# Rotary half turn of the A mixers: from one full-precision product to two one-pass products of parts, with the turn between the halves of the next input piece

## The chip, the cores and the metric

The kernel is one program on one core of a Trainium2 chip. The metric is the device time in microseconds, from repeated executions; a second, separate execution was recorded by the hardware profiler. The engines each run their own queue of instructions in order, and meet at semaphores: TensorE (PE: matmuls, with PEld for its weight loads), VectorE (DVE), ScalarE (ACT), GpSimd (POOL) and SyncE (SP, which issues DMAs).

## The reference, cut to what matters

A stack of fourteen stages on 256 tokens of width 1024 (feed-forwards, a recurrent hybrid, an mLSTM, and attention mixers). The change touches the two differential attention mixers, called A here. Their computation:

```python
def apply_rope(x, cos, sin):                      # on q and k, 16 half heads of 64
    x1, x2 = jnp.split(xf, 2, axis=-1)
    return jnp.concatenate([x1 * c - x2 * s, x2 * c + x1 * s], axis=-1)

def diff_attention(h, w_in, w_out, lam_params, subln_g, cos, sin, layer_idx):
    q, k, v = jnp.split(h @ w_in, [nq, 2 * nq], axis=-1)
    q = apply_rope(...); k = apply_rope(...)
    p = softmax(where(causal, q @ k * scale, -inf))           # two per head
    o = (p[:, :, 0] - lam * p[:, :, 1]) @ v
    o = rms_norm_2(o, subln_g) * (1.0 - lam_init)
    return o.reshape(...) @ w_out
```

The rotation needs, beside x, its half turn: the vector (-x2, x1) within each 64 rows. The kernel makes it as a product with a constant 128x128 matrix of 0, 1 and -1, `turn`.

## The kernel before, in words

**Exactness by parts.** A float32 product on TensorE takes several passes. The kernel mostly splits each float32 operand into a high part of type fp32r, which goes through in one pass, and a low part (the value minus its high part), and sums three one-pass products. For the weights, ScalarE makes the high part (`hi`, L625) and VectorE the low part (`lo_ahead`, L1262). The half turn (L2450) is an exception: it takes the float32 matrix and the float32 values directly.

**The weight stream.** Weights come in pieces of 128x2048 through three slots: SyncE loads piece n when the low part of piece n-3 is made; ScalarE makes its high part when TensorE is done with piece n-3, VectorE then its low part. ScalarE and VectorE work on piece k+2 when their queue reaches the step of piece k.

**An A mixer** has 12 input pieces (8 with queries or keys, each a pair of heads, 4 with values) and 4 output pieces. TensorE projects a piece into one of three banks (`project`; a value piece in `values`), ScalarE copies the result out (`evacuate`), two buffers `raw_qk` in turn. TensorE turns it into the bank MISC (`turn_pair`), and VectorE rotates: raw x cos (L1665), turned x sin (L1668), their sum (L1682), which it signals with `roped`.

**The order of the work** is one string per kind of mixer, `ATTENTION`, walked by TensorE, ScalarE and VectorE alike; each engine puts into its own queue what it has to do at a step. Numbers are pieces, rotations or units (heads):
- `in` k: TensorE projects piece k; ScalarE makes the high part of piece k+2, then copies piece k out; VectorE makes the low part of piece k+2. `fst` and `snd` (used by the C mixer only, before) are the halves: TensorE projects columns 0 to 127 or 128 to 255; ScalarE's high part stands at `fst` and its copy at `snd`.
- `rot` k: TensorE turns, VectorE rotates. The turn waits for the copy, for the rotation before (`roped`) and for the outputs read from MISC.
- `S` u: TensorE computes scores of unit u (it waits for `roped` of the pair's query and key, for example S2 for rotation 3, and for the exponentials of unit u-1); VectorE finds the row maxima (L1734 to L1743, "mask" below); ScalarE makes the exponentials (L916).
- `N` u: VectorE makes the softmax weights (L1753 to L1771) from the exponentials.
- `T` u: TensorE transposes them, ScalarE copies (L926). `W` u: TensorE weighs the values into MISC (L2535, L2536), after waiting for every rotation issued so far; ScalarE copies out (L882).
- `sq`, `sum`, `ln`, `nrm`, `D`, `hi`, `lo`: the norm of the outputs and the output projection.

GpSimd has no work in an A mixer; in the B mixer it makes one high part a unit (L607).

Of the kernel before, what the change touches and what calls it, by code (L numbers as in the profile page):

```python
# [55 lines left out]
for _name, _rows in ROWS:  # L56
# [15 lines left out]
WEIGHTS_MOVE = {"A": 4, "B": 4, "C": 4}  # L72
LATE_LOW = {"A": (), "B": (6, 8), "C": ()}
ATTENTION = {
    "A": """in0 in1 in2 rot0 in3 rot1 in4 S0 rot2 in5 S1 rot3 N0 in6 S2 T0 rot4 N1 in7 W0 S3 T1 rot5 N2 in8 W1 S4 T2 rot6
            N3 in9 W2 S5 T3 rot7 N4 sq0 in10 W3 S6 T4 sum0 N5 ln0 nrm0 sq1 in11 T5 sum1 W4 S7 N6 ln1 D0.0 W5 sq2 hi0 D0.1
            nrm1 T6 N7 D0.2 D0.3 lo0 sum2 W6 ln2 D1.0 D1.1 nrm2 T7 D1.2 D1.3 hi1 lo1 W7 sq3 D2.0 D2.1 sum3 ln3 nrm3
            D2.2 D2.3 hi2 lo2 D3.0 D3.1 D3.2 D3.3 hi3 lo3""",
    "B": """in0 in1 in2 scale0 in3 scale1 U0 in4 in5 scale2 U1 in6 scale3 low8 U2 in7 scale4 U3 in8 scale5 low10 U4 in9 U5 in10 scale6
# [86 lines left out]
def build(nc, a, out, stages):  # L166
# [13 lines left out]
    with ExitStack() as ctx:  # L180
        def sb(name, shape, dt=F32):
            return ctx.enter_context(nc.sbuf_tensor(name, shape, dt))

        def sem(name):
            return ctx.enter_context(nc.semaphore(name))
# [44 lines left out]
        sp_r = sb("sp_r", [P, 4, 384], F32R)  # L230
        sp_hi, sp_lo = sp_r[:, 0:2, :], sp_r[:, 2:4, :]
        pick_r = sb("pick_r", [P, SSD_H], F32R)
        rows_r = sp_r[:, :, :].rearrange("p a c -> p (a c)")[:, 0:2 * T]
        sinks = sb("sinks", [P, 16])
        lam = sb("lam", [P, 2])
# [158 lines left out]
        ln_ready = sem("ln_ready")  # L394
        sp_ready = sem("sp_ready")
        nb_ready = sem("nb_ready")
        sph_ready = sem("sph_ready")
        spl_ready = sem("spl_ready")
        r_ready = sem("r_ready")
        arg_ready = sem("arg_ready")  # L400
# [148 lines left out]
        @block.gpsimd  # L549
        def _(pool):  # L550
            nchain = [0]

            def link(ins):
                nchain[0] += 1
                ins.then_inc(pool_chain, 1)
                pool.wait_ge(pool_chain, nchain[0])

            link(pool.memset(ident[:, :], 0.0))
            pool.memset(ones[:, :], 1.0).then_inc(const_ready, 1)
            pool.memset(eps_c[:, :], EPS).then_inc(const_ready, 1)  # L560
            pool.affine_select(out=ident[:, :], in_=ident[:, :], compare_op=ALU.not_equal, fill=1.0, base=0,
                               pattern=[[-1, P]], channel_multiplier=1).then_inc(const_ready, 1)


            for t in (causal, later):
                link(pool.memset(t[:, :], 1.0))
            for t in (turn, a_mask, c_mask):
                link(pool.memset(t[:, :], 0.0))
            halves = turn[:, :].rearrange("p (h c) -> p h c", h=2)

            def keep(view, op, fill, base, pattern, multiplier):
                link(pool.affine_select(out=view, in_=view, compare_op=op, fill=fill, base=base,
                                        pattern=pattern, channel_multiplier=multiplier))

            keep(causal[:, 0:256], ALU.is_ge, 0.0, 0, [[1, 256]], -1)
            keep(causal[:, 256:384], ALU.is_ge, 0.0, 0, [[1, P]], -1)
            keep(later[:, :], ALU.is_gt, 0.0, 0, [[-1, P]], 1)
            keep(halves[:, :, 0:32], ALU.not_equal, -1.0, -32, [[-64, 2], [-1, 32]], 1)
            keep(halves[:, :, 32:64], ALU.not_equal, 1.0, 0, [[-64, 2], [-1, 32]], 1)
            keep(a_mask[:, 0:256], ALU.is_ge, -1e30, 128, [[-1, 256]], 1)  # L580
            keep(a_mask[:, 256:384], ALU.is_ge, -1e30, 0, [[-1, P]], 1)
            keep(c_mask[:, 0:128], ALU.is_gt, -1e30, 0, [[1, P]], -1)
            keep(c_mask[:, 128:256], ALU.is_ge, -1e30, 0, [[-1, P]], 1)
            keep(c_mask[:, 256:384], ALU.is_ge, -1e30, 0, [[-1, P]], 1)
            link(pool.memset(blocks[:, :], 1.0))
            keep(blocks[:, :], ALU.is_ge, 0.0, 0, [[-4, 32]], 1)
            keep(blocks[:, :], ALU.is_ge, 0.0, 3, [[4, 32]], -1)
            pool.memset(sub_mark[:, :], 0.0).then_inc(masks_ready, 1)
            if plan.subs:
                pool.wait_ge(first_used, 2 * KT - 2)  # L590
                for i, piece in enumerate(ada_pieces):
                    for x in range(2):
                        if i:
                            pool.wait_ge(ada_chain, 2 * (i - 1) + x + 1)
                        pool.dma_start(ada_w[:, x, :], a["ada"][2 * (piece - 8) + x]).then_inc(ada_loaded[x], 16)  # L595


            for st in plan.steps:
                if st["key"][0] == "B":
                    for kind, u in sequence("B"):  # L600
                        if kind != "U":
                            continue
                        if u < 8:
                            pool.wait_ge(sp_ready, u + 1)
                            if u:
                                pool.wait_ge(r_ready, u)
                            pool.tensor_copy(sp_hi, sp).then_inc(sph_ready, 1)  # L607


        @block.scalar  # L610
        def _(act):
# [239 lines left out]
            def evacuate(st, i):  # L851

                kind, n = st["key"][0], st["piece"] + i
                act.wait_ge(piece_used, n + 1)
                b = io(n)
                if kind == "C" and i == 0:
                    act.activation(raw_part(kind, 0)[:, 0, :], b[:, 0, :], ACT.Copy).then_inc(proj_ready, 1)
                    return
                if i in VALUE_PIECES[kind]:
                    if i % 2:  # L860
                        p = VALUE_PIECES[kind][i]
                        for x in range(TB):
                            act.activation(V[:, x, 512 * p:512 * p + 512], IO[(n - 1 + x) % RING][:, :],
                                           ACT.Copy, scale=r_col[:, x:x + 1]).then_inc(proj_ready, 1)
                    return
                rot = ROT_PIECE[kind].index(i)
                query = kind == "C" or rot % 2 == 0
                if kind == "B":
                    j = rot // 2
                    dst = (Q if query else K)[:, 2 * j:2 * j + 2, :]  # L870
                else:
                    buffers = 4 if kind == "C" else 2
                    if rot >= buffers:
                        act.wait_ge(roped, st["rots"] + rot - buffers + 1)
                    dst = raw_part(kind, rot)
                act.activation(dst, b, ACT.Copy, scale=0.125 if query else 1.0).then_inc(proj_ready, 1)

            def outputs(st, u):
# [365 lines left out]
        def _(dve):  # L1244
# [449 lines left out]
            def stick_unit(st, u):  # L1694
# [8 lines left out]
                if u < 8:  # L1703
                    dve.wait_ge(ln_ready, u + 1)
                    if u:
                        dve.wait_ge(spl_ready, u)
                    banks = score_banks(st, u)
                    for h in range(2):
                        ins = dve.scalar_tensor_tensor(out=sp[:, h, :], in0=banks[h][:, 0:384], scalar=0.0,
                                                       in1=lnv[:, h, :], op0=ALU.max, op1=ALU.add)  # L1710
                    ins.then_inc(sp_ready, 1)
                    if u >= 2:
                        dve.wait_ge(o_ready, st["att"] + u - 1)
                    w = nb[:, u % 2, :, :]
                    for h in range(2):
                        ins = dve.scalar_tensor_tensor(out=w[:, h, :], in0=banks[h][:, 0:384], scalar=0.0,
                                                       in1=lnv[:, h, :], op0=ALU.min, op1=ALU.subtract)
                    ins.then_inc(nb_ready, 1)
                    dve.wait_ge(sph_ready, u + 1)
                    if u:  # L1720
                        dve.wait_ge(r_ready, u)
                    dve.tensor_tensor(sp_lo, sp, sp_hi.bitcast(F32), ALU.subtract).then_inc(spl_ready, 1)
# [64 lines left out]
            def attention(st):  # L1787
                kind, n0 = st["key"][0], st["piece"]
                for step, k in sequence(kind):
                    if step == "in" or (step, k) == ("fst", 2):  # L1790
                        if k not in LATE_LOW[kind]:
                            lo_ahead(n0 + k + 2)
                    elif step == "low":
# [387 lines left out]
            def lambda_columns():  # L2181
# [2 lines left out]
                dve.tensor_copy(later_r[:, :], later[:, :])  # L2184
                dve.tensor_copy(ones_r[:, :], ones[:, 0:4])
                link(dve.tensor_copy(ident_r[:, :], ident[:, :]))
                for i in range(2):
                    link(dve.tensor_tensor(lam[:, i:i + 1], lam_s[:, 2 * i + 1:2 * i + 2], lam_s[:, 2 * i:2 * i + 1],
                                           ALU.subtract))
# [29 lines left out]
        def _(pe):  # L2219
# [216 lines left out]
            def turn_pair(st, k, units):  # L2436
# [10 lines left out]
                elif kind == "C":  # L2447
                    pe.wait_ge(ot_ready, st["att"])
                m = MISC[:, 0:nt * T].rearrange("p (t n) -> p t n", t=nt)
                pe.matmul(m, turn[:, :], raw_part(kind, k)[:, 0:nt, :], start=True, stop=True).then_inc(turned, 1)  # L2450

            def scores(st, u):
# [572 lines left out]
```

## Time and profile before

| what | us |
|---|---|
| median of 3 runs | 2405.68 |
| lowest and highest | 2403.62, 2410.78 |
| the profiled execution's own time | 2406.78 |
| its span, first to last instruction | 2404.7 |
| busy: PE, DVE, ACT, POOL | 2345.0, 1718.7, 1192.0, 80.7 |
| granted TensorE clock, mean | 0.997 of full |

The span lies 2.1 us inside the profiled execution's time, and that time is 1.1 us above the median. An instruction's row gives its start and its duration; on TensorE, matmuls overlap, so the time that one takes is read from the start of the next. In brackets stands how long the engine was idle before it, and who ended the wait. The first A mixer lies between about 1172 and 1300 us, the second between about 2088 and 2210.

### The profile page before, as it was taken

How to read it: one execution, taken by the hardware profiler on the slowest of the kernel's cores; microseconds unless marked ns; L12 is line 12 of the kernel's file. 1: busy time of each engine (PE TensorE's matmuls, PEld its weight loads, DVE VectorE, ACT ScalarE, POOL GpSimd, SP SyncE). 2: the span in 40 equal slices, each digit the busy share in tenths (PEclk: the TensorE clock that was granted, in tenths of full speed). 3: DMA queues.
4: the chain of work that ended last, by engine and by line, in shares of the span. 5: the costliest groups of instructions: out<-in, count | busy, mean ns of one | idle time of the engine just before them, and what ended most of it. 6: DMA issues, size and time to landing. Idle time of an engine off the chain costs nothing.

```text
span 2404.7 us, 46561 instructions
## 1 busy us (share of the span) xinstructions
PE 2345.0 (98%) x19290; PEld 2259.5 (94%) x19290; DVE 1718.7 (71%) x2260; ACT 1192.0 (50%) x1489; POOL 80.7 (3%) x163
## 2 busy tenths in 40 slices
PE   6999999999999999999999999999999999999999
PEld 6999988999999989999988999899997899988999
DVE  7888788777877867655677666676667666677665
ACT  5335865334434655433556435654345633546434
POOL 1110000010010000000000000000000000000000
PEclk9999999999999999999999999999999999999999
DMA  8987465787788433455433554436542355443652
GB/s 342 326 314 264 158 217 204 279 295 267 273 297 289 175 135 111 172 194 191 172 123 124 208 192 158 148 116 209 193 175 79 123 204 193 156 153 111 210 192 105
DMA packets 75561, 471.62 MB, mean 196 GB/s; under 512 B 8632, under 2 KB 9144, under 8 KB 26808
## 3 DMA queue, kind: packets, MB, share of 16 engines
q1 hardware_dynamic: 56288, 400.79, 46.5%
q0 software_dynamic: 18432, 67.12, 7.9%
q10 hardware_dynamic: 728, 2.14, 0.3%
q8 instruction: 80, 1.31, 0.2%
q14 instruction: 33, 0.27, 0.0%
HBM read 468.96 MB, written 1.05 MB: 195 GB/s over the span
## 4 chain that ended last, share of the span: by engine, by line
PE 80%; DVE 10%; ACT 4%; DMA 4%; issue 2%; POOL 0%; ACTq 0%; DVEq 0%; POOLq 0%
PE bank L2222 23%; PE bank L2223 23%; PE bank L2224 23%; DVE w_lo L1262 2%; DMA ada_wbuf<-in_ada 2%; PE bank L2228 2%; DVE ada_wbuf L1411 2%; PE bank L2233 2%; PE bank L2229 2%; DMA ARENA<-in_first 1%; ACT w_hi L625 1%; PE bank L2450 1%; PE bank L2484 1%; ACT ARENA L916 0%; DVE ARENA L1734 0%
## 5 line engine op out<-in xcount | busy, mean ns | idle before, releaser
L1262 DVE TENSOR_TENSOR w_lo<-w_raw,w_hi 128x2048 fp32r<-128x2048 f32 x371 | 848.9, 2289 | 319.9 <-ACT w_hi L625 319.1
L625 ACT ACTIVATE w_hi<-w_raw 128x2048 fp32r<-128x2048 f32 x371 | 708.9, 1914 | 508.4 <-PE bank L2224 493.3
L2222 PE MATMUL bank<-h_hi,w_hi 128*128 128x256 f32 x3376 | 944.2, 280 | 1.5 <-DVE w_lo L1262 1.5
L2224 PE MATMUL bank<-h_hi,w_lo 128*128 128x256 f32 x3376 | 935.8, 277 | 0.0
L2223 PE MATMUL bank<-h_lo,w_hi 128*128 128x256 f32 x3376 | 935.8, 277 | 0.0
L2222 PEld LDWEIGHTS bank<-h_hi,w_hi 128*128 128x128 f32 x3376 | 634.7, 188 | 8.3 <-issue 5.1
L2223 PEld LDWEIGHTS bank<-h_lo,w_hi 128*128 128x128 f32 x3376 | 634.8, 188 | 3.5 <-issue 3.3
L2224 PEld LDWEIGHTS bank<-h_hi,w_lo 128*128 128x128 f32 x3376 | 634.6, 188 | 0.0
L2222 PE MATMUL bank<-d_hi,w_hi 128*128 128x256 f32 x1920 | 536.3, 279 | 4.1 <-DVE d_lo L1639 4.0
L2224 PE MATMUL bank<-d_hi,w_lo 128*128 128x256 f32 x1920 | 532.2, 277 | 0.0
L2223 PE MATMUL bank<-d_lo,w_hi 128*128 128x256 f32 x1920 | 532.1, 277 | 0.0
L2222 PEld LDWEIGHTS bank<-d_hi,w_hi 128*128 128x128 f32 x1920 | 360.6, 188 | 7.7 <-DVE d_lo L1639 5.5
L2223 PEld LDWEIGHTS bank<-d_lo,w_hi 128*128 128x128 f32 x1920 | 360.6, 188 | 0.5 <-issue 0.5
L2224 PEld LDWEIGHTS bank<-d_hi,w_lo 128*128 128x128 f32 x1920 | 360.5, 188 | 0.0
L1411 DVE CUSTOM_DVE_ANT_0 ada_wbuf<-ada_wbuf,c_rows 128x1024 f32<-128x1024 f32 x128 | 155.7, 1219 | 31.1 <-DMA ada_wbuf<-in_ada 31.1
L2228 PE MATMUL bank<-h_hi,w_hi 128*128 128x256 f32 x440 | 111.7, 286 | 3.2 <-ACT h_hi L676 2.8
L816 ACT ACTIVATE gate_s<-gate_s 128x512 f32<-128x512 f32 x44 | 27.9, 633 | 170.6 <-DVE gate_s L1572 170.6
L2229 PE MATMUL bank<-h_hi,w_lo 128*128 128x256 f32 x440 | 109.3, 281 | 0.0
L595 POOL DMA_DIRECT2D ada_wbuf<-in_ada x128 | 67.8, 530 | 786.0 <-DVE ada_sum L1411 756.2
L2228 PEld LDWEIGHTS bank<-h_hi,w_hi 128*128 128x128 f32 x440 | 83.5, 190 | 9.4 <-issue 7.7
L789 ACT ACTIVATE gate_s<-bank 128x512 f32<-128x512 f32 x40 | 24.0, 600 | 137.1 <-PE bank L2224 134.8
L1593 DVE CAST d_hi<-hid 128x512 fp32r<-128x512 f32 x88 | 37.5, 426 | 73.8 <-PE bank L2224 73.3
(407 smaller groups left out, 2271.9 us busy)
## 6 DMA issues: line engine op xcount, KB each, us to landing
w_raw<-in_ws SPq DMA_DIRECT2D x371, 1024.0 KB, 4.8
ada_wbuf<-in_ada POOLq DMA_DIRECT2D x128, 512.0 KB, 5.3
ARENA<-in_first SPq DMA_DIRECT2D x8, 1024.0 KB, 19.8
work<-in_x SPq DMA_DIRECT2D x1, 1024.0 KB, 11.3
ARENA<-in_wax ACTq DMA_DIRECT2D x1, 1024.0 KB, 4.8
out_y<-ARENA SPq DMA_DIRECT2D x4, 256.0 KB, 2.2
ARENA<-in_wg ACTq DMA_DIRECT2D x1, 768.0 KB
c_rows<-in_c SPq DMA_DIRECT2D x1, 512.0 KB, 4.9
```

The costliest lines, as they stand in the source:

```text
L595: pool.dma_start(ada_w[:, x, :], a["ada"][2 * (piece - 8) + x]).then_inc(ada_loaded[x], 16)
L625: act.activation(w_hi[:, slot, :], w_raw[:, slot, :], ACT.Copy).then_inc(hi_ready, 1)
L816: act.activation(gate_s[:, :, :], gate_s[:, :, :], ACT.Silu).then_inc(silu_ready, 1)
L1262: dve.tensor_tensor(w_lo[:, s, :], w_raw[:, s, :], w_hi[:, s, :].bitcast(F32), ALU.subtract).then_inc(lo_ready, 1)
L1411: dve.tensor_tensor_reduce(out=w, in0=w, in1=c_rows[:, :], scale=1.0, scalar=0.0, op0=ALU.mult, op1=ALU.add, accum_out=dst).then_inc(ada_c ...
L1593: dve.tensor_copy(d_hi[:, buf, :, :], hid[:, :, :]).then_inc(dve_chain, 1)
L2222: pe.matmul(o, whi, xhi, start=start, stop=False, skip_group_check=True)
L2223: pe.matmul(o, whi, xlo, start=False, stop=False, skip_group_check=True)
L2224: return pe.matmul(o, wlo, xhi, start=False, stop=stop, skip_group_check=True)
L2228: pe.matmul(o, whi, xhi, start=start, stop=False, skip_group_check=True)
L2229: pe.matmul(o, wlo, xhi, start=False, stop=False, skip_group_check=True)
L2233: return pe.matmul(o, whi, xlo, start=False, stop=stop, skip_group_check=True)
```

## The change

The eight rotations of an A mixer work on parts. ScalarE copies each query or key piece twice out of its bank: once as float32, as before, and once rounded to fp32r (the high part). GpSimd subtracts the high part from the float32 copy (the low part). TensorE multiplies an fp32r copy of the matrix, `turn_r`, with the high part and then with the low part, one pass each, into the same bank. The parts lie in `sp_r`, the B mixer's scratch: two buffers for the high part, one for the low part. The order string changes from piece 5 to piece 9: these pieces are projected in halves, and turns 2 to 6 stand between them (turn 2 inside piece 5 and so on); turn 7 stays behind T3. VectorE's low part of piece k+2 is issued at `fst` k, and N0 now stands ahead of rotation 3. One semaphore is renamed, since both kinds of mixer count on it.

```diff
--- before.py
+++ after.py
@@ -72,8 +72,8 @@
 WEIGHTS_MOVE = {"A": 4, "B": 4, "C": 4}
 LATE_LOW = {"A": (), "B": (6, 8), "C": ()}
 ATTENTION = {
-    "A": """in0 in1 in2 rot0 in3 rot1 in4 S0 rot2 in5 S1 rot3 N0 in6 S2 T0 rot4 N1 in7 W0 S3 T1 rot5 N2 in8 W1 S4 T2 rot6
-            N3 in9 W2 S5 T3 rot7 N4 sq0 in10 W3 S6 T4 sum0 N5 ln0 nrm0 sq1 in11 T5 sum1 W4 S7 N6 ln1 D0.0 W5 sq2 hi0 D0.1
+    "A": """in0 in1 in2 rot0 in3 rot1 in4 S0 fst5 rot2 snd5 S1 fst6 N0 rot3 snd6 S2 T0 fst7 rot4 N1 snd7 W0 S3 T1 fst8 rot5 N2 snd8
+            W1 S4 T2 fst9 rot6 N3 snd9 W2 S5 T3 rot7 N4 sq0 in10 W3 S6 T4 sum0 N5 ln0 nrm0 sq1 in11 T5 sum1 W4 S7 N6 ln1 D0.0 W5 sq2 hi0 D0.1
             nrm1 T6 N7 D0.2 D0.3 lo0 sum2 W6 ln2 D1.0 D1.1 nrm2 T7 D1.2 D1.3 hi1 lo1 W7 sq3 D2.0 D2.1 sum3 ln3 nrm3
             D2.2 D2.3 hi2 lo2 D3.0 D3.1 D3.2 D3.3 hi3 lo3""",
     "B": """in0 in1 in2 scale0 in3 scale1 U0 in4 in5 scale2 U1 in6 scale3 low8 U2 in7 scale4 U3 in8 scale5 low10 U4 in9 U5 in10 scale6
@@ -230,6 +230,8 @@
         sp_r = sb("sp_r", [P, 4, 384], F32R)
         sp_hi, sp_lo = sp_r[:, 0:2, :], sp_r[:, 2:4, :]
         pick_r = sb("pick_r", [P, SSD_H], F32R)
+        turn_r = sb("turn_r", [P, P], F32R)
+        raw_parts = sp_r[:, :, :].rearrange("p a c -> p (a c)").rearrange("p (x t n) -> p x t n", x=3, t=2)
         rows_r = sp_r[:, :, :].rearrange("p a c -> p (a c)")[:, 0:2 * T]
         sinks = sb("sinks", [P, 16])
         lam = sb("lam", [P, 2])
@@ -394,7 +396,7 @@
         ln_ready = sem("ln_ready")
         sp_ready = sem("sp_ready")
         nb_ready = sem("nb_ready")
-        sph_ready = sem("sph_ready")
+        gpsimd_part = sem("gpsimd_part")
         spl_ready = sem("spl_ready")
         r_ready = sem("r_ready")
         arg_ready = sem("arg_ready")
@@ -596,6 +598,13 @@
 
 
             for st in plan.steps:
+                if st["key"][0] == "A":
+                    for k in range(8):
+                        pool.wait_ge(proj_ready, st["evac"] + ROT_PIECE["A"][k] + 1)
+                        if k:
+                            pool.wait_ge(turned, st["rots"] + k)
+                        pool.tensor_tensor(raw_parts[:, 2, :, :], raw_part("A", k), raw_parts[:, k % 2, :, :].bitcast(F32),
+                                           ALU.subtract).then_inc(gpsimd_part, 1)
                 if st["key"][0] == "B":
                     for kind, u in sequence("B"):
                         if kind != "U":
@@ -604,7 +613,7 @@
                             pool.wait_ge(sp_ready, u + 1)
                             if u:
                                 pool.wait_ge(r_ready, u)
-                            pool.tensor_copy(sp_hi, sp).then_inc(sph_ready, 1)
+                            pool.tensor_copy(sp_hi, sp).then_inc(gpsimd_part, 1)
 
 
         @block.scalar
@@ -873,6 +882,11 @@
                     if rot >= buffers:
                         act.wait_ge(roped, st["rots"] + rot - buffers + 1)
                     dst = raw_part(kind, rot)
+                if kind == "A":
+                    act.activation(dst, b, ACT.Copy, scale=0.125 if query else 1.0)
+                    if rot > 1:
+                        act.wait_ge(turned, st["rots"] + rot - 1)
+                    dst = raw_parts[:, rot % 2, :, :]
                 act.activation(dst, b, ACT.Copy, scale=0.125 if query else 1.0).then_inc(proj_ready, 1)
 
             def outputs(st, u):
@@ -1716,7 +1730,7 @@
                         ins = dve.scalar_tensor_tensor(out=w[:, h, :], in0=banks[h][:, 0:384], scalar=0.0,
                                                        in1=lnv[:, h, :], op0=ALU.min, op1=ALU.subtract)
                     ins.then_inc(nb_ready, 1)
-                    dve.wait_ge(sph_ready, u + 1)
+                    dve.wait_ge(gpsimd_part, 8 + u + 1)
                     if u:
                         dve.wait_ge(r_ready, u)
                     dve.tensor_tensor(sp_lo, sp, sp_hi.bitcast(F32), ALU.subtract).then_inc(spl_ready, 1)
@@ -1787,7 +1801,7 @@
             def attention(st):
                 kind, n0 = st["key"][0], st["piece"]
                 for step, k in sequence(kind):
-                    if step == "in" or (step, k) == ("fst", 2):
+                    if step == "in" or (step == "fst" and (kind == "A" or k == 2)):
                         if k not in LATE_LOW[kind]:
                             lo_ahead(n0 + k + 2)
                     elif step == "low":
@@ -2184,6 +2198,7 @@
                 dve.tensor_copy(later_r[:, :], later[:, :])
                 dve.tensor_copy(ones_r[:, :], ones[:, 0:4])
                 link(dve.tensor_copy(ident_r[:, :], ident[:, :]))
+                link(dve.tensor_copy(turn_r[:, :], turn[:, :]))
                 for i in range(2):
                     link(dve.tensor_tensor(lam[:, i:i + 1], lam_s[:, 2 * i + 1:2 * i + 2], lam_s[:, 2 * i:2 * i + 1],
                                            ALU.subtract))
@@ -2447,6 +2462,11 @@
                 elif kind == "C":
                     pe.wait_ge(ot_ready, st["att"])
                 m = MISC[:, 0:nt * T].rearrange("p (t n) -> p t n", t=nt)
+                if kind == "A":
+                    pe.wait_ge(gpsimd_part, 16 * st["key"][1] + k + 1)
+                    pe.matmul(m, turn_r[:, :], raw_parts[:, k % 2, :, :], start=True, stop=False)
+                    pe.matmul(m, turn_r[:, :], raw_parts[:, 2, :, :], start=False, stop=True).then_inc(turned, 1)
+                    return
                 pe.matmul(m, turn[:, :], raw_part(kind, k)[:, 0:nt, :], start=True, stop=True).then_inc(turned, 1)
 
             def scores(st, u):
```

## Rows read from the trace of the kernel before

**Rows 1.** Page, part 1: busy us of each engine, share of the span, instructions.

```profile
PE 2345.0 (98%) x19290; PEld 2259.5 (94%) x19290; DVE 1718.7 (71%) x2260; ACT 1192.0 (50%) x1489; POOL 80.7 (3%) x163
```

**Rows 2.** Waits of PE, 1180 to 1262: waiter <- releaser: total, times, longest.

```profile
PE bank L2450 <- ACT scrap L839: 0.6, 1, 0.6
```

**Rows 3.** Timeline of PE: start, duration, instruction; value piece, then a turn.

```profile
1192.55 0.40 PE L2223 MATMUL bank<-w_lo,h_hi 128*128 128x512 f32 x1
1192.78 0.40 PE L2224 MATMUL bank<-w_hi,h_lo 128*128 128x512 f32 x1
...
1205.71 1.02 PE L2450 MATMUL bank<-ARENA,turn 128*128 128x512 f32 x2
...
1206.68 0.28 PE L2223 MATMUL bank<-h_lo,w_hi 128*128 128x256 f32 x1
1206.81 0.28 PE L2224 MATMUL bank<-h_hi,w_lo 128*128 128x256 f32 x1
```

**Rows 4.** Timeline of ACT: copies of pieces 0, 1 and 4; first exponentials.

```profile
1183.60 1.08 ACT L876 ACTIVATE ARENA<-bank 128x512 f32<-128x512 f32 x2 [3.60 <-PE bank L2233]
...
1204.62 0.60 ACT L876 ACTIVATE ARENA<-bank 128x512 f32<-128x512 f32 x1 [3.43 <-PE bank L2224]
1207.30 0.47 ACT L916 ACTIVATE ARENA<-bank,ARENA 128x256 f32<-128x256 f32 x1 [2.08 <-DVE ARENA L1743]
```

**Rows 5.** Timeline of POOL in the B mixer: its cast.

```profile
1516.21 0.82 POOL L607 CAST sp_r<-ARENA 128x768 fp32r<-128x768 f32 x1 [653.74 <-DVE ARENA L1709]
```

**Rows 6.** DVE timeline: mask 0, low 7; rotation 3, N0, low 8, mask 2.

```profile
1205.91 1.15 DVE L1734 TENSOR_REDUCE ARENA<-bank 128x1 f32<-128x256 f32 x4 [2.40 <-PE bank L2489]
...
1210.85 2.29 DVE L1262 TENSOR_TENSOR w_lo<-w_raw,w_hi 128x2048 fp32r<-128x2048 f32 x1 [1.66 <-ACT w_hi L625]
...
1214.97 0.69 DVE L1665 TENSOR_TENSOR ARENA<-ARENA,hid 128x512 f32<-128x512 f32 x1
...
1216.91 0.17 DVE L1753 RECIPROCAL ARENA<-ARENA 128x4 f32<-128x4 f32 x1
...
1218.65 2.29 DVE L1262 TENSOR_TENSOR w_lo<-w_raw,w_hi 128x2048 fp32r<-128x2048 f32 x1
...
1221.51 1.15 DVE L1734 TENSOR_REDUCE ARENA<-bank 128x1 f32<-128x256 f32 x4 [0.57 <-PE bank L2489]
```

**Rows 7.** Timeline of DVE: mask 3, low 10, mask 4.

```profile
1230.30 1.15 DVE L1734 TENSOR_REDUCE ARENA<-bank 128x1 f32<-128x256 f32 x4 [1.18 <-PE bank L2489]
...
1235.63 2.29 DVE L1262 TENSOR_TENSOR w_lo<-w_raw,w_hi 128x2048 fp32r<-128x2048 f32 x1 [0.33 <-ACT w_hi L625]
...
1239.09 1.15 DVE L1734 TENSOR_REDUCE ARENA<-bank 128x1 f32<-128x256 f32 x4 [1.17 <-PE bank L2489]
```

**Rows 8.** Timeline of PE: W0, S3 and T1, one after the other.

```profile
1228.16 0.59 PE L2535 MATMUL bank<-ARENA 128*128 128x256 f32 x2
...
1228.90 0.71 PE L2484 MATMUL bank<-ARENA 64*128 64x256 f32 x4
...
1230.10 0.49 PE L2559 MATMUL bank<-ident,ARENA 128*128 128x128 f32 x3
```

**Rows 9.** PE behind three waits, and windows with busy us and granted clock (PEclk).

```profile
41.10 0.74 PE L2233 MATMUL bank<-h_lo,w_hi 128*128 128x256 f32 x4 [2.67 <-DVE h_lo L1483]
...
1844.03 1.52 PE L2559 MATMUL bank<-ident,ARENA 128*128 128x128 f32 x6 [2.33 <-issue]
...
1854.62 0.85 PE L2559 MATMUL bank<-ident,ARENA 128*128 128x128 f32 x6 [1.57 <-ACT ARENA L885]
...
42.00:43.00 1.00, 1.00 (x7) 1.00 (x6) 0.55 (x2) 0.98 (x2) 0.00 (x0) 0.50 1.01 410
...
1844.00:1845.00 1.00, 0.97 (x5) 1.00 (x6) 1.00 (x3) 0.00 (x0) 0.00 (x0) 0.50 0.01 0
...
1847.00:1848.00 1.00, 1.00 (x7) 0.44 (x4) 1.00 (x4) 1.00 (x7) 0.00 (x0) 0.83 0.00 0
...
1855.00:1856.00 1.00, 1.00 (x14) 0.83 (x13) 1.00 (x3) 0.00 (x0) 0.00 (x0) 1.00 0.00 0
```

## The prediction

> **What bounds the kernel now.** The page first: TensorE is busy for 98% of the span, VectorE for 71% [rows 1]. So a TensorE microsecond taken away is worth one, and so is a TensorE wait that is added. The change touches the two A mixers only; I read the first from its timelines, and take the second as equal (its mask steps stand at the same spacing). Then the waits of TensorE in its first 82 us: one, of 0.6 us, at the first turn [rows 2]. From there past piece 9 it never waits: every other engine has slack there, and the question is how much of it the new order uses up.
>
> **The turn on TensorE.** Before, a turn runs as two instructions that begin at 1205.71; the third matmul behind it begins at 1206.68, and matmuls of this kind follow at 0.12, so the turn took 1206.68 - 0.12 - 1205.71 = 0.85 us. A one-pass product with 512 columns is in the trace: in the value pieces they follow each other at 0.23 us [rows 3]. Two of them cost 0.47. That saves 0.38 a turn, 16 turns: **6.1 us, if nothing waits**. Cutting a piece into halves costs nothing: the same matmuls in the same order, one turn between them.
>
> **ScalarE and GpSimd.** Each of the 16 copies out of the bank is made a second time: 0.60 us by its row [rows 4]. For pieces 4 to 9 it lies in ScalarE's idle time ahead of the next mask (2.1 us idle before the exponentials at 1207.30). The one place where it shows is piece 0: piece 2 may enter bank 0 only when the parts of piece 0 are copied, and here ScalarE goes straight from the end of piece 1 to them; I charge 0.5 us a stage (bounds 0 and 0.6). The subtraction on GpSimd has no row. Nearest: its cast of 768 columns, 0.83 us [rows 5]. 512 columns of one input would be 0.55, doubled for a second input 1.1; I take 1.1, being the nearer case, with 0.55 and 2.3 (as slow as VectorE's subtraction of 2048 columns) for the range. The part is there 0.2 + 0.6 + 0.6 + 0.1 + 1.1 = 2.6 us after the piece ends; the turn comes a score and a half piece later, 1.2 + 2.8 = 4.0. Hidden for turns 2 to 6; at 2.3 us it would be just hidden. Turn 7 keeps its old place behind piece 9 and 2.3 us of other work, and would wait 0.3; but TensorE waits ahead of it anyway (below). The copy of the turning matrix and the renamed semaphore: nothing.
>
> **The move that decides: VectorE's queue.** The order string is walked by all engines. On VectorE an opening half now issues the low part of weight piece k+2, so "S0 fst5 rot2" means mask 0, low 7, rotation 2, where it was mask 0, rotation 2, low 7. Low 7 waits for high 7 from ScalarE, and that stands behind the exponentials of mask 0, which wait for the mask. Before, rotation and softmax weights filled this hole. Now they stand behind it. Terms, start to start [rows 6]: mask to low part 1210.85 - 1205.91 = 4.94; low part 2.20 (2.29 long, 0.09 overlapped); rotation 1216.91 - 1214.97 = 1.94; weights N 1218.65 - 1216.91 = 1.74.
>
> First leg, counted from the start of mask 0. TensorE is never late for S1 (mask 1 may start as soon as VectorE is free): low 7 at 4.94, rotation 2 at 7.14, mask 1 at 9.08, low 8 at 14.02, N0 at 16.22, rotation 3 at 17.96, done at 19.9. S2 needs rotation 3. TensorE would be at S2 after fst, turn, snd, S1, fst, turn, snd, about 13.2: **it waits 6.7 us**. S2 takes 1.20 and a signal 0.2: mask 2 at 21.4. Before it was at 1221.51 - 1205.91 = 15.6. **Lost: 5.8.**
>
> Then three equal cycles. With the transposes in ScalarE's queue, mask to low part is 1235.63 - 1230.30 = 5.33 [rows 7]. Then low part 2.20, rotation 1.94, signal 0.1; W (the weighing with values) waits for all rotations issued so far, so W is next, 0.74, and S 1.20 [rows 8], signal 0.2: 11.7 us from mask to mask, with N beside W and S. Before: 1239.09 - 1230.30 = 8.79. **Lost: 2.9 a cycle, 3 cycles (S2 to S5), 8.8**, as waits of about 3.3 us ahead of W0, W1 and W2. TensorE's savings on turns 2 to 6 only lengthen these waits. After S5 the order is the old one, TensorE sets the pace again.
>
> Per stage: 5.8 + 8.8 + 0.5 at piece 2 - 3 x 0.38 (turns 0, 1, 7) = 14.0; two stages: **+28 us**.
>
> **The clock.** Eight waits of TensorE, two of 6.7 and six of 3.3, are new. The trace has two waits of that size in its running part: 2.67 us before 41.10 and 2.33 before 1844.03. Behind both the granted clock is 0.50, the 1.2 GHz level; the second time it begins with the work at 1844.0 and ends in the window 1847 to 1848, whose mean of 0.83 puts the end at 1847.3 (a third of that window at half), some 3.3 us; after the wait of 1.57 before 1854.62 it stays at 1.00 [rows 9]. Behind W0 and W1, W and S (1.94 us) lie in VectorE's loop, and at half clock with a start 0.5 late they cost 1.4 more; S2 costs 0.7 more; behind W2 TensorE is the bound again and loses 1.7. Sum 0.7 + 1.4 + 1.4 + 1.7 = 5.2 a stage if all four gaps bring it, 10.4 in two. I take three quarters, **8 us**, since 3.3 is not far from the 1.57 that brought none. The Trainium skill (TensorE: Matmul & The Clock Gate, "What's actually happening") says that the lowered clock is the default and sustained activity releases it; by that rule all eight gaps are candidates (+10.4), and the trace agrees at the two gaps named.
>
> **Sum.** The profiled execution took 2406.8 (span 2404.7); 2406.8 + 28 + 8 = 2442.8. It lies 1.1 above the median of the runs, so against 2405.7: **2441 us**, slower by 1.5%.
>
> **Rivals.**
> (a) The waits come, the clock stays up: 2405.7 + 28 = 2434. For: gaps around 3.3 us are rare in this trace and could fall either way; against: both comparable ones brought it. 0.25.
> (b) The two engines get in each other's way: the subtraction starts about 1.4 us after a half piece ends, which in the three cycles is when VectorE adds up the rotation, on the path. If one waits for the other's 1.1 us, six times: +6.6, 2448. The trace can't tell: GpSimd's casts [rows 5] stand beside VectorE instructions that read a bank. The Trainium skill (SBUF — State Buffer, "Who interferes with whom") states that a VectorE instruction with two SBUF inputs and a GpSimd one that reads SBUF exclude each other; it speaks for this rival and nothing in the sum uses it. 0.10.
> (c) Not slower: the hole is no hole. If ScalarE's high part were ready before the mask, the chain mask, low part, rotation, W, S would be 1.3 + 2.2 + 1.9 + 0.1 + 0.7 + 1.2 + 0.2 = 7.6, under TensorE's 8.4 a cycle, and only the turns count: 2405.7 - 6.1 + 1.0 = 2400.6. It decides where the wait for the high part falls under 1.7 us instead of 4.0. For it: VectorE still idles for 0.6 to 1.7 us ahead of single instructions [rows 6]. Against: the high part is queued behind the exponentials, and the low parts in rows 6 and 7 already wait on it. 0.09, a third of it with some further gain.
> (d) Something longer than all this, above 2452: 0.05.
> The forecast has 0.51.
>
> **Numbers.** 0.3% is 7.2 us, about what can be told from no change. Even the full saving of 6.1 is below it, so faster gets 0.03, same 0.06, slower 0.91. The range leaves out (c) and (d): low 2427, which is (a) with one microsecond less in each loop; high 2452, which is (b) with all gaps at half clock.
>
> **What would show it.** Right: waits of TensorE at S2 (near 6.7 us) and W0 to W2 (near 3) on VectorE's rotation add, masks 2 to 5 some 11.7 to 13 apart, VectorE idle about 4 us ahead of low 9, 10 and 11 on ScalarE's high part, turns of 0.47. Wrong: if TensorE waits instead at the turns, for GpSimd, the parts are the bound; if the masks stay 8.8 apart, (c) holds; if the waits are there and the clock row is at 1.00 behind them, (a).

## The result: 2452.2 us against 2405.1, slower by 1.85%

| | before | after |
|---|---|---|
| median of the runs, us | 2405.13 (4 runs) | 2452.16 (4 runs, 2447.33 to 2455.82) |
| ratio, 95% interval | | 1.0185 (1.0171 to 1.0198) |
| span of the profiled execution, us | 2404.7 | 2454.0 |
| first A stage, us | 111.5 | 133.9 |
| second A stage, us | 111.1 | 132.8 |

A stage is measured from one sum of squares to the next: the product of `work` with ones that ends the first pieces of the stage, to that of the feed-forward behind it. The two stages hold 22.4 + 21.7 = 44.1 us of the 47.0. The rest of the run between them is equal (802.7 and 802.3 us). In the profiled execution the first A stage also begins 5.6 us later, 1189.2 against 1183.6. The profiled executions of the experiments have this start anywhere from 1180.5 to 1187.9, ahead of anything that the change issues but one small copy, so I count no part of it for the change.

The page's busy line, to be held against [rows 1]: no engine has more than 24 us of new work, TensorE's busy time rises by 12 in a span longer by 49, and its share falls to 96%.

```profile
PE 2356.9 (96%) x19290; PEld 2273.1 (93%) x19290; DVE 1727.3 (70%) x2261; ACT 1199.6 (49%) x1505; POOL 104.4 (4%) x179
```

The waits of TensorE after, 1180 to 1290 (waiter <- releaser: total, times, longest), where [rows 2] had 0.6 us in all. L2504 is S2, L2555 are W0 to W2, L1696 is the add that ends a rotation on VectorE; L2467 is turn 0:

```profile
PE bank L2555 <- DVE ARENA L1696: 10.8, 3, 4.5
PE bank L2504 <- DVE ARENA L1696: 7.7, 1, 7.7
PE bank L2467 <- issue: 0.5, 1, 0.5
```

TensorE after, a turn between the halves of piece 5, then S2 behind its wait, and the ends of the stage. The turn is 0.47 long (1213.64 to 1214.11), where [rows 3] had 0.85:

```profile
1189.22 1.03 PE L2335 MATMUL bank<-work,ones 128*128 128x256 f32 x4
...
1213.64 0.40 PE L2467 MATMUL bank<-sp_r,turn_r 128*128 128x512 f32 x1
1213.87 0.40 PE L2468 MATMUL bank<-sp_r,turn_r 128*128 128x512 f32 x1
1214.11 0.28 PE L2237 MATMUL bank<-h_hi,w_hi 128*128 128x256 f32 x1
...
1232.25 1.23 PE L2504 MATMUL bank<-ARENA 64*128 64x256 f32 x4 [7.74 <-DVE ARENA L1696]
...
1323.11 1.03 PE L2342 MATMUL bank<-work,ones 128*128 128x256 f32 x4
```

VectorE after, first A stage. L1748 opens a mask, L1276 is a low part, L1696 the rotation's add, L1679 its first product, L1778 two small products in N:

```profile
1211.01 1.15 DVE L1748 TENSOR_REDUCE ARENA<-bank 128x1 f32<-128x256 f32 x4 [2.01 <-PE bank L2509]
...
1215.95 2.29 DVE L1276 TENSOR_TENSOR w_lo<-w_raw,w_hi 128x2048 fp32r<-128x2048 f32 x1 [3.59 <-ACT w_hi L634]
...
1219.48 1.07 DVE L1696 TENSOR_TENSOR ARENA<-ARENA 128x512 f32<-128x512 f32 x1
...
1227.82 1.08 DVE L1778 TENSOR_TENSOR ARENA<-ARENA,lam 128x1 f32<-128x1 f32 x2
...
1234.67 1.15 DVE L1748 TENSOR_REDUCE ARENA<-bank 128x1 f32<-128x256 f32 x4 [2.47 <-PE bank L2509]
...
1239.99 2.29 DVE L1276 TENSOR_TENSOR w_lo<-w_raw,w_hi 128x2048 fp32r<-128x2048 f32 x1 [3.97 <-ACT w_hi L634]
...
1243.52 1.43 DVE L1696 TENSOR_TENSOR ARENA<-ARENA 128x512 f32<-128x512 f32 x1
...
1247.71 1.15 DVE L1748 TENSOR_REDUCE ARENA<-bank 128x1 f32<-128x256 f32 x4 [1.04 <-PE bank L2509]
...
1256.56 1.71 DVE L1696 TENSOR_TENSOR ARENA<-ARENA 128x512 f32<-128x512 f32 x1
...
1268.18 1.78 DVE L1679 TENSOR_TENSOR ARENA<-ARENA,hid 128x512 f32<-128x512 f32 x1
```

The reader is to see three things. Mask to low part is 4.94 and 5.32 us, as in [rows 6, 7], but now VectorE idles 3.6 to 4.0 of it, on ScalarE's high part. Masks 2 and 3 are 13.04 apart, where [rows 7] had 8.79. Masks 4 and 5 are 14.75 apart, which is outside the 11.7 to 13 of the prediction; there the product of 1.78 and the half clock come together. And some instructions are far longer than before: 1.07, 1.43 and 1.71 for an add that always took 0.69, as all 20 of it in the kernel before show (min, median, max in ns):

```profile
L1682 DVE TENSOR_TENSOR ARENA<-ARENA x20: 691/692/694, 1193.5 to 2164.4; 128x512 f32<-128x512 f32 x20
```

GpSimd after: the subtractions of the parts. The one at 1243.15 ends at 1244.41, and the add that began beside it at 1243.52 ends at 1244.95, 0.54 behind it:

```profile
1218.29 1.72 POOL L606 TENSOR_TENSOR sp_r<-ARENA,sp_r 128x512 fp32r<-128x512 f32 x1 [6.11 <-ACT sp_r L890]
...
1243.15 1.26 POOL L606 TENSOR_TENSOR sp_r<-ARENA,sp_r 128x512 fp32r<-128x512 f32 x1 [14.33 <-ACT sp_r L890]
...
1268.15 1.26 POOL L606 TENSOR_TENSOR sp_r<-ARENA,sp_r 128x512 fp32r<-128x512 f32 x1 [10.42 <-ACT sp_r L890]
```

Windows after (busy us of each engine, PEclk, DMA share, GB/s), to be held against [rows 9]: half clock at S2, full again at 1237; half clock behind W2 as well.

```profile
1234.00:1235.00 1.00, 1.00 (x6) 1.00 (x6) 0.33 (x1) 0.00 (x0) 0.00 (x0) 0.50 0.00 0
1237.00:1238.00 1.00, 1.00 (x11) 1.00 (x10) 0.00 (x0) 1.00 (x6) 0.00 (x0) 1.00 0.00 0
1273.00:1275.00 2.00, 2.00 (x11) 1.62 (x10) 0.00 (x1) 0.38 (x1) 0.00 (x0) 0.50 0.00 0
```

### The profile page after: what moved, and what is told of

It reads as the page before. It is cut to its first block, busy times and chain, and to the rows that moved or that the text cites. A ratio compares the mean times of both kernels' runs of the same rounds, so it can differ in the third digit from the quotient of the medians.

```text
span 2454.0 us, 46618 instructions
## 1 busy us (share of the span) xinstructions
PE 2356.9 (96%) x19290; PEld 2273.1 (93%) x19290; DVE 1727.3 (70%) x2261; ACT 1199.6 (49%) x1505; POOL 104.4 (4%) x179
## 4 chain that ended last, share of the span: by engine, by line
PE 74%; DVE 12%; ACT 5%; DMA 4%; issue 4%; POOL 0%; ACTq 0%; DVEq 0%; POOLq 0%
PE bank L2237 21%; PE bank L2239 21%; PE bank L2238 21%; DMA ada_wbuf<-in_ada 3%; DVE w_lo L1276 3%; DVE ada_wbuf L1425 2%; ACT w_hi L634 2%; PE bank L2243 2%; PE bank L2248 2%; PE bank L2244 1%; DMA ARENA<-in_first 1%; ACT ARENA L930 1%; DVE ARENA L1748 1%; PE bank L2504 1%; DVE ARENA L1696 0%
## 5 line engine op out<-in xcount | busy, mean ns | idle before, releaser
L1276 DVE TENSOR_TENSOR w_lo<-w_raw,w_hi 128x2048 fp32r<-128x2048 f32 x371 | 848.9, 2289 | 356.3 <-ACT w_hi L634 355.4
```

Of the source, the lines that this page charges most:

```text
L1276: dve.tensor_tensor(w_lo[:, s, :], w_raw[:, s, :], w_hi[:, s, :].bitcast(F32), ALU.subtract).then_inc(lo_ready, 1)
```

## Experiments

The stage lengths of every profiled execution, first and second A stage, by the same two products; the difference is against 111.5 and 111.1. Each length comes from one profiled execution. The two stages of a kernel agree within 0.4 us, but for the changed kernel and the one with no read on GpSimd (1.1 and 1.3), whose half clock falls differently in the two, while the whole run spreads by up to 11.5 us; so the small effects are read from the stages.

| kernel | median us (ratio to before, interval) | A stages, us | both, against before |
|---|---|---|---|
| after | 2452.2 (1.0185, 1.0171 to 1.0198) | 133.9, 132.8 | +44.1 |
| order alone | 2442.5 (1.0151, 1.0135 to 1.0168) | 129.2, 129.1 | +35.7 |
| no read on GpSimd | 2441.4 (1.0141, 1.0126 to 1.0155) | 129.9, 128.6 | +36.0 |
| waits filled | 2438.6 (1.0136, 1.0118 to 1.0155) | 128.0, 128.1 | +33.5 |
| parts alone | 2416.2 (1.0036, 1.0023 to 1.0049) | 114.6, 114.6 | +6.6 |
| low part at the second half | 2405.4 (0.9996, 0.9986 to 1.0007) | 110.2, 110.4 | -2.0 |
| high part early | 2406.0 (0.9998, 0.9987 to 1.0009) | 110.8, 111.0 | -0.8 |
| parts for six turns | 2402.96 (0.9989, 0.9978 to 0.9999) | 109.1, 109.1 | -4.4 |

**The order alone.** The kernel before, with the diff's string and its VectorE step; no parts.

```diff
-                    if step == "in" or (step, k) == ("fst", 2):
+                    if step == "in" or (step == "fst" and (kind == "A" or k == 2)):
```

> The kernel before with only the new order string and the low part at the first half; the turn is the float32 product of 0.85 us, one copy by ScalarE, nothing on GpSimd. Theory 1: nearly all of the loss is here: waits of 6 at S2 and 2.9 at W0 to W2 a stage, 2 x 14.6 = 29 us, and 4 to 8 us of half clock behind them: 2434 to 2442. Rival (order and parts each carry a share): under 2425.

Measured 2442.5, half a microsecond above the 2434 to 2442 expected. Its waits of TensorE, 1180 to 1330:

```profile
PE bank L2535 <- DVE ARENA L1682: 7.2, 3, 2.9
PE bank L2484 <- DVE ARENA L1682: 5.7, 1, 5.7
```

The order alone loses 35.7 us without a single part. S2 waits 5.7 where the kernel with parts and no read on GpSimd (below) waits 6.5, and W1 and W2 2.9 where that one waits 3.3: two turns and one turn that are 0.38 longer fill the difference. The rest, up to the 7.7 of the changed kernel, is the meeting of GpSimd and VectorE.

**The parts alone.** The changed kernel with the old string (the diff's lines of the string taken back).

> The changed kernel with the order string of before: whole pieces, each turn directly behind one score. Parts by ScalarE and GpSimd stay. The part is ready 0.2 + 0.6 + 0.6 + 0.1 + 1.3 = 2.8 us after the piece, TensorE is at the turn after 1.2 (turns 2 and 3), 1.5 (turn 4) and 2.3 us (turns 5 to 7): waits of 1.6, 1.6, 1.2, 0.5, 0.5, 0.5, and 0.5 at piece 2, in sum 6.4 a stage, less 8 x 0.38 = 3.1: 2 x 3.3 = +6.5, 2411.5 us. Rival (the parts are the dear side of the change): above 2425. Other rival (GpSimd's part comes in time): 2400.

Stages +6.6, which is the expected sum; the median is +9.2, and the interval of the ratio holds 5.5 to 11.8 us. The single waits came out shorter than expected, 4.7 in all for 5.9, so the sum agrees partly by luck, and about 1 us a stage is not accounted for. Its waits of TensorE, 1200 to 1262:

```profile
PE bank L2467 <- POOL sp_r L606: 4.7, 6, 1.3
```

Behind one score, the part comes late. So the halves were needed; what was wrong was what else the string moved.

**The low part at the second half.** The changed kernel, one line of VectorE's.

```diff
-                    if step == "in" or (step == "fst" and (kind == "A" or k == 2)):
+                    if step == "in" or (step, k) == ("fst", 2) or (step == "snd" and kind == "A"):
```

> The changed kernel with one edit: VectorE makes the low part of piece k+2 at the second half of piece k, so behind rotation and softmax weights, as in the kernel before; turns, parts and halves stay. Theory 1 (VectorE's queue makes the waits): the waits at S2 and W0 to W2 are gone, masks 8.4 us apart, 12 turns of 0.47 hidden by nothing; only a second copy at piece 2 (+0.5 a stage) and turn 7's wait for GpSimd (+0.5 a stage) remain: 2405.1 - 6.1 + 2.0 = about 2401 us, under the kernel before by 0.1 to 0.25%. Rival (the parts are the cost, through GpSimd and the second copy): the waits stay in good part, at the turns instead, and the time stays above 2430. If VectorE and GpSimd hold each other up as in the changed kernel, it is slack that pays, and the time is still near 2401.

2405.4: the whole loss is gone, by one step of VectorE's queue, the low part, moved behind others. The gain is -2.0 where -4.1 was expected. The missing 2.1 us is one wait, of turn 7, 1.5 us a stage where 0.5 was expected. In its trace the subtraction for turn 7 starts 0.94 us into a low part and then takes 2.5 us (VectorE, GpSimd, and the wait of TensorE, 1200 to 1262):

```profile
1244.32 2.28 DVE L1276 TENSOR_TENSOR w_lo<-w_raw,w_hi 128x2048 fp32r<-128x2048 f32 x1
```

```profile
1245.26 2.47 POOL L606 TENSOR_TENSOR sp_r<-ARENA,sp_r 128x512 fp32r<-128x512 f32 x1 [5.89 <-ACT sp_r L890]
```

```profile
PE bank L2467 <- POOL sp_r L606: 1.5, 1, 1.5
```

The low part ends at 1246.60; 1.13 us later, at 1247.73, the subtraction is done, a little under its undisturbed length of 1.26. The subtractions for turns 5 and 6 are as long (2.50 and 2.51), but TensorE does not wait for them.

**The high part early.** The changed kernel, VectorE's order and all; ScalarE makes its high part behind the copy instead of behind the exponentials.

```diff
                     elif step == "fst":
-                        hi_ahead(n0 + k + 2)
+                        if kind != "A":
+                            hi_ahead(n0 + k + 2)
                     elif step == "snd":
                         evacuate(st, k)
+                        if kind == "A" and k < 9:
+                            hi_ahead(n0 + k + 3)
```

and the same for piece 7 behind the copy of piece 4.

> The changed kernel, VectorE's order and all; only ScalarE makes its high parts earlier: that of piece k+3 right behind its copy of piece k, so ahead of the exponentials, for pieces 7 to 11. VectorE's low part at the first half then finds its high part ready. Theory (what opens the hole in VectorE's queue is the high part behind the exponentials, as the rival of the prediction that would have ended not slower has it): the chain mask, low, rotation, W, S is 7.7 us, under TensorE's 8.4, the waits at S2 and W0 to W2 are gone: about 2405. Rival (the low part ahead of the rotation costs by its own 2.2 us too): waits of 1 us or so stay at W0 to W2, 2410 to 2415.

2406.0, and masks 8.4 us apart (VectorE, masks 3 and 4 and the low part between them; here no wait for the high part is left, and ahead of low parts 7 and 8 it is 0.3):

```profile
1231.69 1.15 DVE L1753 TENSOR_REDUCE ARENA<-bank 128x1 f32<-128x256 f32 x4 [1.21 <-PE bank L2514]
1232.95 2.29 DVE L1281 TENSOR_TENSOR w_lo<-w_raw,w_hi 128x2048 fp32r<-128x2048 f32 x1
...
1240.08 1.15 DVE L1753 TENSOR_REDUCE ARENA<-bank 128x1 f32<-128x256 f32 x4 [1.20 <-PE bank L2514]
```

A wait of 1.5 us on the rotation stays at S2, which the expectation did not have. So the low part ahead of the rotation does little harm by its own 2.2 us. The harm was that it waited.

**No read on GpSimd.** GpSimd writes zeros and reads nothing from SBUF.

```diff
-                        pool.tensor_tensor(raw_parts[:, 2, :, :], raw_part("A", k), raw_parts[:, k % 2, :, :].bitcast(F32),
-                                           ALU.subtract).then_inc(gpsimd_part, 1)
+                        pool.memset(raw_parts[:, 2, :, :].bitcast(F32), 0.0).then_inc(gpsimd_part, 1)
```

> The changed kernel, but GpSimd fills the low part with zeros instead of subtracting: it reads nothing from SBUF, and the low half of the turn is left out of the result. Same order, same signals. Theory 2 (the subtraction and VectorE's instructions with two SBUF inputs hold each other up, 4.1 us in the first A stage by the lengthened rows: adds of 1.07, 1.43 and 1.71, a product of 1.78 where 0.69 is normal, small products of 1.08 for 0.23): every one of these rows is back at its normal length and the time falls by about 8 us, to 2444. Rival (the lengthened rows come from elsewhere, such as the DMA stream, or are made up for by the waits): they stay, or the time moves by under 2 us. The waits at S2 and W0 to W2 stay in either case, near 6.5 and 3.0.

2441.4 where 2444 was expected; the stages are shorter than those of the changed kernel by 8.1 in all, which is the 8 expected. The rotation's add, all 20 of it (min, median, max in ns), and the waits of TensorE, 1180 to 1330:

```profile
L1695 DVE TENSOR_TENSOR ARENA<-ARENA x20: 691/692/694, 1191.7 to 2198.0; 128x512 f32<-128x512 f32 x20
```

```profile
PE bank L2554 <- DVE ARENA L1695: 9.2, 3, 3.3
PE bank L2503 <- DVE ARENA L1695: 6.5, 1, 6.5
```

In the changed kernel the longest was 1712. The fill is shorter than the subtraction, 0.52 us, but it too runs beside this add (from 2167.30 and 2192.12), and the add keeps its length. The theory stands. Its size is 8.1 us of the 44.1 by the stages, and 7.0 by the lengthened rows, 4.1 in the first stage and 2.9 in the second (small products of 1.08; adds of 1.07, 1.04, 1.23 and 1.48). The 1.1 us between the two is not isolated: the half clock falls at other places in each execution.

**The waits filled.** The changed kernel with idle products ahead of its four waits a stage.

```diff
+            def fill(n):
+                for _ in range(n):
+                    pe.matmul(PS[3][:, 0:T], ident[:, :], causal[:, 0:T], start=True, stop=True)
...
+                    if kind == "A" and (step, k) == ("S", 2):
+                        fill(15)
+                    elif kind == "A" and step == "W" and k < 3:
+                        fill(6)
```

> The changed kernel with float32 products of two constants put into TensorE's queue ahead of S2 (15 of 0.43 us) and ahead of W0, W1 and W2 (6 of 0.43 us), into a bank that nothing uses there, so that TensorE is not idle while it waits for the rotation. Nothing else changes, no result does. Theory (the half clock behind the waits costs 3.4 us in the loops of the first A stage by its rows, and about as much after the last wait and in the second stage): the granted clock stays at 1.00 in both A stages and the time falls by 6 to 9 us against the changed kernel, to 2443 to 2446, with VectorE's rotation still the releaser. Rival (the clock costs nothing, since the work behind a wait has slack): 2452, the clock at 1.00 or not. If the filling is longer than the waits it adds time, by its rows at most 1 us a stage.

2438.6: 13.6 less than the changed kernel by the medians, 11.8 by the ratios to the kernel before, 10.6 by the stages; all are more than the 6 to 9 expected. The clock stays up where W0 and S3 run, and W0 waits for what the fill left over:

```profile
1237.00:1239.00 2.00, 1.80 (x13) 1.51 (x14) 1.66 (x8) 0.39 (x1) 0.00 (x0) 1.00 0.94 393
```

```profile
1237.19 0.67 PE L2555 MATMUL bank<-ARENA 128*128 128x256 f32 x2 [1.04 <-DVE ARENA L1696]
```

Not all of it is clock. The meeting of GpSimd and VectorE also fell otherwise: the lengthened rows of the first stage add 2.3 us here (adds of 1.07 and three of 1.04, small products of 1.09), against 4.1 in the changed kernel. That leaves 5.9 - 1.8 = 4.1 us of clock in the first stage. The second has the same 2.3 against 2.9, and leaves 4.7 - 0.6 = 4.1 too.

**Parts for six turns.** The kernel with the low part at the second half; turns 0 and 7 go back to one copy and the float32 product.

```diff
-                if kind == "A":
-                    pe.wait_ge(gpsimd_part, 16 * st["key"][1] + k + 1)
+                if kind == "A" and 0 < k < 7:
+                    pe.wait_ge(gpsimd_part, 14 * st["key"][1] + k)
```

with the same condition at ScalarE's second copy and in GpSimd's loop.

> The kernel with the low part at the second half (2405.4 against 2407.0), and turns 0 and 7 made as before, with the float32 product and one copy. In its trace turn 7 waits 1.5 us for GpSimd's part, and piece 2 waits 0.5 us for the second copy of piece 0; each of these turns saves 0.38 as parts. Theory: a stage gains 1.5 - 0.38 + 0.5 - 0.38 = 1.3 us on it, two stages 2.5: 2402.9, and against the kernel before -2.0 - 2.5 = -4.5 us (0.9981). Rival: the waits only pass on to the next ones, S5 to S6 or the value pieces: no difference from 2405.4.

Stages -4.4, where -4.5 was expected, and median 2402.96. The ratio says less: 0.9989 where 0.9981 was expected. Its interval, 0.9978 to 0.9999, holds the expected one and just leaves out no change. Its waits of TensorE, 1190 to 1262, hold none for GpSimd:

```profile
PE bank L2469 <- ACT scrap L847: 0.6, 1, 0.6
PE bank L2554 <- ACT ARENA L871: 0.4, 1, 0.4
```

It is the fastest version found, and the gain is small: 12 turns at 0.38 are 4.6 us.

## Why the prediction was right, and where it fell short

**The step that decided held.** VectorE's queue was laid out from start-to-start times, and those that nothing disturbed came back to 0.1 us: 4.94 and 5.33 forecast from mask to low part, 4.94 and 5.32 measured; turns of 0.47; piece 2 later by 0.4 (forecast 0.5); GpSimd's subtraction 1.26 undisturbed (1.1). Waits at S2 of 6.7 forecast, 7.7 measured; W0 to W2 3.3 forecast, 3.2, 3.2 and 4.5 measured. Where GpSimd reads nothing they are 6.5 and, at the longest, 3.3, so the method was right. That the changed kernel's 3.2 are as near is in part luck: the longer adds make the waits longer, and TensorE's work between them, up to 10.2 us long with the half clock in place of 8.7, makes them shorter. The turns' savings did lengthen the waits and gave nothing. The rival "not slower" named the point of decision, and the kernel with the high part early shows it: the hole closed, the loss is gone.

**The forecast of 2441 was 11 us low.** The term that failed is the meeting of GpSimd and VectorE. I had it as a rival, (b), at +6.6 us and a chance of 0.10, and left it out of the sum. It is worth 8.1 us by the stages: 0.4 and 0.8 in the first leg, 0.7, 1.0 and 1.1 in the three cycles make 4.1 in the first stage. The rival had six meetings in the cycles, at 1.1 each; there were also two in each first leg, and only one of the ten cost the full 1.1. The reason given for the low chance, that no row of before showed it, was a reason for not knowing and no reason against. With it the sum is 2449. So what happened is the forecast's wait and its clock together with rival (b), and the measured 2452.2 lies at the very top of the range, 2427 to 2452. That end was called (b) with all gaps at half clock; its own terms, 2448 + 2.4, give 2450. The Trainium skill (SBUF — State Buffer, "Who interferes with whom") says that the pair of ports is an exclusive lock, and that the order of issue decides who is held up. The traces agree both ways: the add waited for the subtraction (1.43 for 0.69), and in another kernel the subtraction waited for the low part (2.47 for 1.26).

**The clock.** Forecast 8 us, that is 4.0 a stage. The filled waits give 4.1 for each stage. The zeros on GpSimd fit it but do not measure it: 36.0 us less 2 x 14.0 of forecast waits leaves 8.0 for two stages. The size was right, though three quarters was a guess: the granted clock was at half behind three of the first stage's four waits and all four of the second's, but not always at the start of the work. The comparison with two waits was also thin: in the trace of before the clock is at half within 1.3 us after a wait of 1.88 us (ahead of 869.91), and stays up after one of 1.79 (ahead of 1864.44). The Trainium skill (TensorE: Matmul & The Clock Gate, "What's actually happening") has idleness as the state in which the clock is low, and sustained work releasing it; the filled kernel, at 1.00 throughout these stages, agrees.

**Left open.** The waits of 14.0 a stage are worked out, not isolated: filled waits less the lengthened rows give 16.5 - 2.3 = 14.2 in the first stage and 17.0 - 2.3 = 14.7 in the second. The last 3 us between 2449 and 2452 lie outside the two A stages. In the profiled execution the first of them starts later, and that start differs by up to 8.7 us among the kernels; no run told whether the change has a share.

## What to carry to other kernels

When a queue gets a new order, follow on each engine what the moved instruction itself waits for: an instruction that must wait for another engine belongs behind the work that doesn't. Here one step, the subtraction for the weights' low part, moved ahead of the rotation that had filled its wait, cost six times what the whole change could save. Count a second engine's reads as a cost to the first when both will run at once, even if no row shows it yet. And a stall of TensorE costs more than its length where the clock falls behind it, here about 4 us a stage on top of 14.

## What the runs showed of the hardware

- A GpSimd subtraction of 128x512 takes 1.26 to 1.29 us undisturbed and up to 2.51 beside a VectorE low part; a VectorE add of 0.69 takes up to 1.71 beside it. With a GpSimd fill that reads nothing (0.52 us), every add is back at 0.69.
- Even two VectorE products of one column each took 1.08 instead of 0.23 beside GpSimd's subtraction.
- Of the six waits of TensorE ahead of W0 to W2 in the changed kernel (3.15 to 4.48 us), five were followed by half clock within 1.8 us of the work's start; the one at 1258.42, 3.15 us long, was not. The stretches at half clock lasted from 3.4 to 6.8 us.
